# Moving two of five modulation jobs from the projections into attention, and the order of the weight slabs that goes with it

## The reference

```python
m_lat = jax.nn.silu(c) @ w_mod[l] + b_mod[l]                 # 1024 x 6144: sh1, sc1, g1, sh2, sc2, g2
h = modulate(rmsnorm(x, norm_mix[l]), sh1, sc1)              # needs the first 2048 columns only
proj = h @ w_in[l]                                           # q, k, v, glu, two gates: 1024 x 4608
att = latent_neighbourhood_attention(q, k, v, k_c, v_c, rpb[l])
y = merge_branches(proj, att, conv_w, ..., w_att_out, w_conv_out, w_o)
x_mid = x + g1 * y
...
mod = silu(c_2) @ w_ada_2[l] + b_ada_2[l]                    # second block's six vectors, 1024 x 6144
```

## Time and profile before

| | us |
|---|---|
| median of 3 runs | 3107.19 (3105.99 to 3111.87) |
| the profiled execution | 3105.99 |
| its span in the profile | 3104.0 |
| first job of the kernel starts on TensorE | 36.00 |
| attention starts | 264.50 |
| merge starts | 367.53 |
| TensorE busy | 2247.8 |
| VectorE busy | 1420.5 |

### The profile page before, as it was taken

One profiled execution on the slowest core, in us unless ns is written; L12 is line 12 of the kernel. 1 busy time (PEld: TensorE's weight loads), 2 busy tenths in 40 slices (PEclk: granted clock), 3 DMA queues, 4 the chain that ended last, 5 costly groups with the idle time before them and its releaser, 6 DMA issues.

```text
span 3104.0 us, 28552 instructions
## 1 busy us (share of the span) xinstructions
PE 2247.8 (72%) x9662; PEld 967.5 (31%) x9662; DVE 1420.5 (46%) x3317; ACT 703.3 (23%) x1672; POOL 596.9 (19%) x593
## 2 busy tenths in 40 slices
PE   2998899858877774799778986547765655665554
PEld 1443544433322221354557543212211111111110
DVE  1394411320000002201258566666677777777765
ACT  2003411110000101302146443212222222232222
POOL 1000000010000001000012222243443444444442
PEclk8999999869999997889788688768878777777777
DMA  8348519449999996422036856899999999999996
GB/s 256 126 168 292 207 67 216 191 162 401 404 412 410 412 414 237 163 81 82 28 134 248 323 230 267 314 372 400 417 419 421 421 421 421 421 403 422 421 421 266
DMA packets 216905, 922.69 MB, mean 297 GB/s; under 512 B 19266, under 2 KB 59280, under 8 KB 125902
## 3 DMA queue, kind: packets, MB, share of 16 engines
q0 software_dynamic: 79056, 552.76, 43.8%
q1 hardware_dynamic: 127936, 359.68, 31.4%
q10 hardware_dynamic: 9790, 8.73, 0.8%
HBM read 889.32 MB, written 31.78 MB: 297 GB/s over the span
## 4 chain that ended last, share of the span: by engine, by line
DMA 31%; PE 27%; DVE 12%; issue 4%; ACT 4%; POOL 1%; SPq 0%; DVEq 0%; POOLq 0%; ACTq 0%
DMA ring<-in_expert_pair,ids 16%; DMA ring<-in_w_exp_up 11%; PE bank L1883 7%; PE bank L2423 5%; PE bank L2105 5%; DVE ring L1832 4%; PE bank L1889 3%; DMA arena_v<-in_expert_pair,ids 1%; DMA pair_last<-in_expert_pair,ids 1%; PE bank L2436 1%; ACT arena_w L1277 1%; DMA ring<-in_w_exp_down 1%; PE bank L2239 1%; PE bank L2238 1%; DVE pair_last L1832 1%
## 5 line engine op out<-in xcount | busy, mean ns | idle before, releaser
L2423 PE MATMUL bank<-ring,arena_w 128*32 128x512 f32 x1568 | 552.6, 828 | 360.9 <-ACT arena_w L1277 360.9
L873 POOL DMA_INDIRECT ring<-in_expert_pair,ids x392 | 421.4, 1075 | 1139.1 <-PE bank L2423 706.5
L1883 PE MATMUL bank<-arena_h,ring 128*128 128x512 f32 (+1 forms) x1024 | 372.4, 524 | 4.9 <-ACT arena_h L916 2.5
L2105 PE MATMUL bank<-ring,arena_h 128*64 128x512 f32 x1056 | 272.7, 675 | 81.3 <-DMA ring<-in_w_exp_up 74.5
L2423 PEld LDWEIGHTS bank<-ring,arena_w 128*32 128x32 f32 x1568 | 94.3, 132 | 675.4 <-ACT arena_w L1277 507.9
L1832 DVE CUSTOM_DVE_ANT_0 ring<-ring,arena_h 128x1024 f32<-128x1024 f32 x203 | 245.7, 1226 | 126.2 <-DMA ring<-in_expert_pair,ids 91.4
L1832 DVE CUSTOM_DVE_ANT_0 ring<-ring 128x1024 f32<-128x1024 f32 x189 | 229.6, 1225 | 76.9 <-DMA ring<-in_expert_pair,ids 68.3
L1883 PEld LDWEIGHTS bank<-arena_h,ring 128*128 128x128 f32 x1024 | 178.7, 197 | 187.9 <-issue 182.0
L1578 DVE TENSOR_TENSOR arena_q<-arena_q,bank 128x256 f32<-128x256 f32 x32 | 13.5, 421 | 488.7 <-ACT arena_q L1045 488.7
L1275 ACT ACTIVATE arena_w<-arena_w 128x2 f32<-128x2 f32 (+1 forms) x224 | 45.4, 203 | 761.7 <-DVE arena_w L1832 761.4
L2105 PEld LDWEIGHTS bank<-ring,arena_h 128*64 128x64 f32 x1056 | 94.4, 154 | 258.0 <-issue 250.7
(11 more groups left out here) (451 smaller groups left out, 3058.4 us busy)
## 6 DMA issues: line engine op xcount, KB each, us to landing
ring<-in_w_exp_gate SPq DMA_DIRECT2D x33, 2048.0 KB, 19.4
ring<-in_w_exp_up SPq DMA_DIRECT2D x33, 2048.0 KB, 23.6
ring<-in_w_exp_down SPq DMA_DIRECT2D x33, 2048.0 KB, 24.3
ring<-in_w_in SPq DMA_DIRECT2D x15, 2048.0 KB, 19.2
ring<-in_w_mod SPq DMA_DIRECT2D x12, 2048.0 KB, 16.4
ring<-in_w_ada SPq DMA_DIRECT2D x12, 2048.0 KB, 14.8
xs_d<-zeros SPq DMA_DIRECT2D x1, 12032.0 KB, 69.9
arena_h<-xs_d SPq DMA_DIRECT2D x66, 128.0 KB, 23.3
```

Of the source, the lines that this page charges most:

```text
L873: pool.indirect_dma_start(pair[pair_of(m)], None, A["expert_pair_2"], bass.IndirectOffsetOnAxis(ap=ids[n % 2][:, r:r + 1], axis=0)).then_i ...
L1883: mm = pe.matmul(dst, w[:, c, at], rhs[:, c, :], start=(c == 0), stop=(c == chunks - 1))
L2105: mm = pe.matmul(bank[2 + b][at, :].rearrange("p (g f) -> p g f", g=2), xbT[b][:, c, :], gu[:, :, c, 256 * half:256 * half + 256], start=( ...
L2423: mm = pe.matmul(bank[4 + 2 * (n // H % 2) + half][at, :], sel_q[:, n % 2, k0 + j, :], pair[pair_of(m + j)][:, D + 512 * half:D + 512 * ha ...
```

## The change

J0 moves from behind projection 7 to behind projection 10. J1 and J2 leave the projections; the four jobs J1 to J4 stand behind steps 4, 8, 11 and 14 of attention, all in bank 7. The slabs are listed as K, V, Q (6, 7, 8) and then the twenty of the jobs in a row (J0 9 to 12, J1 13 to 16, J2 17 to 20, J3 21 to 24, J4 25 to 28); from 29 on the list is unchanged. VectorE adds J0's bias behind the whole convolution. On GpSimd's queue each later bias load trades places with a store of rows.

```diff
-        jobs = [(cols_pc(A["w_mod"], 4 + j), (DC, 512), pe_mod, 2 + j // 4) for j in range(8)]
-        jobs += [(cols_pc(A["w_ada_2"], j), (DC, 512), pe_mod, 4 + j // 4) for j in range(12)]
-        slabs += [(cols_pc(w_in, QKV + 1), (DC, 512), proj_done, 8)] + jobs[0:4]
-        slabs += [(cols_pc(w_in, QKV + 2), (DC, 512), proj_done, 14)] + jobs[4:8]
-        slabs += [(cols_pc(w_in, QKV), (DC, 512), proj_done, 18)] + jobs[8:20]
+        slabs += [(cols_pc(w_in, QKV + 1), (DC, 512), proj_done, 8), (cols_pc(w_in, QKV + 2), (DC, 512), proj_done, 14),
+                  (cols_pc(w_in, QKV), (DC, 512), proj_done, 18)]
+        slabs += [(cols_pc(A["w_mod"], 4 + j), (DC, 512), pe_mod, 2 + j // 4) for j in range(8)]
+        slabs += [(cols_pc(A["w_ada_2"], j), (DC, 512), pe_mod, 4 + j // 4) for j in range(12)]
...
-        N_JOB = (7, 12, 17, 21, 25)
+        N_MOD, N_GLU, N_K, N_V, N_Q, N_JOB, N_GA, N_WO = 0, 4, 6, 7, 8, 9, 29, 35
...
-        PROJ_JOB, AT_MEAN, AT_VAR, AT_JOB = (7, 13, 17), 0, 2, (4, 9)
-        JOB_BANK = (0, 1, 2, 7, 7)
+        PROJ_JOB, AT_MEAN, AT_VAR, AT_JOB = 10, 0, 2, (4, 8, 11, 14)
...
             bias_rows(0)
             store_rows(0)
+            bias_rows(1)
             store_rows(1)
-            bias_rows(1)
+            bias_rows(2)
             store_rows(2)
-            bias_rows(2)
+            bias_rows(3)
             store_rows(3)
-            bias_rows(3)
             store_rows(4)
...
-                if cc >= 2:
-                    job_rows(cc - 2)
-            job_rows(2)
+            job_rows(0)
...
-                    job_rows(3 + AT_JOB.index(i - 1))
+                    job_rows(1 + AT_JOB.index(i - 1))
...
-                if m in PROJ_JOB:
-                    j = PROJ_JOB.index(m)
+                if m == PROJ_JOB:
                     pe.wait_ge(u_done, CC)
-                    modulation(N_JOB[j], JOB_BANK[j], 0 if j < 2 else 2)
+                    modulation(N_JOB, 0, 0)
...
-                if i == 1:
-                    pe.wait_ge(mod_rows, 4 + 12)
...
-            pe.wait_ge(mod_rows, 4 + 8)
+            pe.wait_ge(mod_rows, 4 + 4)
...
-                    j = 3 + AT_JOB.index(i)
-                    if j == 3:
+                    j = 1 + AT_JOB.index(i)
+                    if j == 1:
                         pe.wait_ge(cms_done, 1)
                     else:
                         pe.wait_ge(mod_rows, 4 + 4 * j)
-                    modulation(N_JOB[j], JOB_BANK[j], 2)
+                    modulation(N_JOB + 4 * j, 7, 0 if j < 2 else 2)
```

More of the change, by code:

```diff
@@ L490, in build @@
         slabs += [(cols_cp(A["w_o"], j), (DC, 512), wo_pe, 8) for j in range(2)]
-        N_MOD, N_GLU, N_K, N_V, N_Q, N_GA, N_WO = 0, 4, 6, 11, 16, 29, 35
-        N_JOB = (7, 12, 17, 21, 25)
+        N_MOD, N_GLU, N_K, N_V, N_Q, N_JOB, N_GA, N_WO = 0, 4, 6, 7, 8, 9, 29, 35
         def w_gu(w, e):
@@ L1390, in job_rows @@
                     dve.wait_ge(*((mod_out_rest, 64 * i) if i <= 2 else (mod2_out, 64 * (i - 2))))
-                dve.tensor_tensor(mod_row, bank[JOB_BANK[i]][:, :], mod_bias[i % 3], ALU.add).then_inc(mod_rows, 4)
+                dve.tensor_tensor(mod_row, bank[7 if i else 0][:, :], mod_bias[i % 3], ALU.add).then_inc(mod_rows, 4)
             dve.wait_ge(convw_T, CC)
```

## The result

Six runs of the changed kernel had a median of 3126.52 us (3119.99 to 3131.48), six of the kernel before one of 3109.53 (3104.42 to 3122.53). The ratio is 1.0055, with a 95% interval from 1.0033 to 1.0078: 17 us, somewhere between 10 and 24. The forecast had the direction (slower, near the bound) and the mechanism, the ring running dry, and it was too small: 3115.0 with a range to 3122. All 23 executions of the changed kernel, seventeen of them outside this comparison, have a median of 3129.77 (3119.99 to 3143.69).

The account below looks back on a forecast made before the run. TensorE, gapless before attention and from the merge on, bounds the kernel, so the merge's start sets the end. Merge 7.5 us late plus 1.5 for the clock, 9.0 on 3105.99, gave 3115.0 us, range 3101 to 3122.

Parts of the forecast that it names:

- the ring running dry: Six-slot ring in attention: late slabs freed only by the preceding job make J3, J4 and merge wait, 12.1 us in all.
- wait ahead of J3, J4, merge: TensorE's waits for late ring loads in attention and at the merge's start: 4.2, 4.2 and 3.7 us.
- the later merge is found again: Behind the merge nothing swallows a shift, so its later start moves the experts and the end by the same amount.
- GpSimd's reordered bias loads cost nothing: Bias loads queued behind row stores in attention: the 1.3 us wait at step 8 lies under J2's 7 us.
- TensorE's clock. I take 1.5 in all: Slow clock behind the three new load waits: bounds 0 and 2.3 us each, 1.5 us taken in all.
- the backlog of loads would partly swallow a slower J3: In attention, a slower J3 is partly swallowed by queued loads; the start of the merge is not.
- I take 15.5: From a job's end to its batch's second slab landing, ahead of J3 and J4: 15.5 us, from readings of 15.5 and 16.7.
- by the backlog: Ahead of the merge: slab 30 lands 26.8 us behind J3, the next two 10.9 us later, at 375.1.
- The sum: Whole kernel: 7.5 + 1.5 = 9.0 us on the profiled execution's 3105.99, giving 3115.0.
- The loads in time: Rival: second slab within 11.3 us, no load waits, merge 4.6 us early, 3101.4; loads in time or nearly, chance 0.22.
- Attention swallowing the jobs: Rival: attention's 26 us of TensorE idle takes the moved jobs, up to 14 us kept, 3092; below 3101, chance 0.08.
- Everything at its upper bound: Rival: longest load times and low-clock jobs, merge 13.5 us late, 3119.5; above 3121 with later stages slower, chance 0.08.

Follow-up runs that it names:

- half: Changed kernel with J2, J3 and J4 loading two slabs each instead of four, same 64 matmuls; ratio 0.9987 to the kernel before, attention stretch 134.47 us.
- shift110: Kernel before with 128 extra unused matmuls directly ahead of the merge; 110.3 us later at the merge, ratio 1.0359.
- shift14: Kernel before with 32 extra unused matmuls directly ahead of the merge; they took 27.7 us, ratio 1.0060.
- warm: Changed kernel with 3, 4 and 6 unused matmuls in the load waits ahead of J3, J4 and the merge; ratio 1.0029 to the kernel before.
- split: Changed kernel with the wait for the two output weights moved behind the merge's first gate matmuls; ratio 1.0029 to the kernel before.
- spaced: Changed kernel with J3 and J4 one step later, behind steps 12 and 15 of attention; ratio 1.0048 to the kernel before.
- one_moved: Kernel before with only J2 moved from the projections into attention, its three jobs there behind steps 4, 8 and 12; ratio 0.9993.
- gap: Kernel before with J2 moved into TensorE's wait ahead of the variance and J3 put behind step 5; ratio 0.9985.

## Why the prediction was right in kind and too small

| step of the forecast | forecast | measured |
|---|---|---|
| attention starts | 250.5 | 250.53 |
| J1, J2 start | 278.5, 307.8 | 278.32, 307.48 |
| J3 could start, starts | 326.1, 330.3 | 327.81, 331.02 |
| wait ahead of J3, J4, merge | 4.2, 4.2, 3.7 | 3.21, 4.13, 6.58 |
| job's end to second slab in use (J3, J4) | 15.5, 15.5 | 16.5, 15.6 |
| J3, J4 last | 7.1, 7.1 | 8.7, 8.7 |
| J4's end to the merge | 15.0 | 15.9 |
| merge starts | 375.0 and a part of 1.5 | 379.90 |
| merge's first 32 matmul records, beyond 14.0 | rest of the 1.5 | 1.4 |
| total | 3115.0 | 3126.52 |

**What held.** The ring running dry, step by step: which slab is held by which job, three waits and none ahead of J1 and J2, the landing 16.4 and 15.4 us behind a job's end. `half` takes only slabs away and all of the loss goes. That the later merge is found again: the first experts' matmul comes at 685.55 and not at 670.61, and in the total `shift110` shows it; `shift14` leaves it open to 9 us. That attention starts at 250.53 and not elsewhere is in part luck (below, third).

That GpSimd's reordered bias loads cost nothing held as well. VectorE does wait for them, twice, which it did not in the kernel before:

```profile
306.43 1.04 DVE L1428 TENSOR_TENSOR arena_w<-spare,band 128x512 f32<-128x512 f32 x1 [1.26 <-DMA spare<-skew_d]
...
330.36 1.02 DVE L1428 TENSOR_TENSOR arena_w<-spare,band 128x512 f32<-128x512 f32 x1 [3.02 <-DMA spare<-skew_d]
...
340.95 0.43 DVE L1439 TENSOR_TENSOR bank<-bank,arena_w 128x256 f32<-128x256 f32 x1 [8.74 <-PE bank L1982]
```

The first wait is the forecast's 1.3 us and lies under J2. (The 0.5 us an issue in that sum is 0.54 rounded down and not up, as it says there; the four stores took 1.95 us.) The second, 3.02 us, lies under TensorE's own wait for J3's slab, and VectorE then waits 8.74 us for TensorE's next scores. `half` has both too (1.16 and 2.51 us), without the loss.

**What failed, first: the term "TensorE's clock. I take 1.5 in all".** It lay between bounds of 0 and 2.3 for each of three waits, so 0 to 6.9, and I chose near the lower end. Measured are 8.77 - 7.07 = 1.7 behind each of the first two waits and 15.36 - 14.00 = 1.4 behind the third: 4.8. The granted clock of the changed kernel in 330 to 340 us, the stretch of J3, with TensorE busy for 9 of 10 us (columns: PE, PEld, DVE, ACT, POOL, PEclk, DMA share, GB/s):

```profile
330.00:340.00 10.00, 8.98 (x66) 3.10 (x68) 1.79 (x3) 0.00 (x0) 0.00 (x0) 0.83 1.04 383
```

0.83 is the mean of a stretch at 1.2 GHz and the rest at 2.4: an estimate from it is a third of the 10 us at the lower level, which costs 1.7 us, as J3 does. The Trainium skill, "TensorE: Matmul & The Clock Gate", section "Part 1: The HAM clock gate", says that the slow clock is the default and that activity releases it; by that `warm`, which only adds activity, should bring the jobs back to their length, and it did (7.07 us). My rows could have said so: the variance had lost 2.28 us behind a wait of 4.93.

I had also argued that the backlog of loads would partly swallow a slower J3. It swallowed nothing: J4's slab 28 is released by J3's end, and J4 starts 15.4 to 16.2 us behind that end in five traces (the changed kernel's two, `split`, `warm`, `spaced`), however late it is.

**Second: what loads took.** "I take 15.5" was the lower of two rows, 15.5 and 16.7. J3 came 16.5 us behind J2's end, 1.0 us more; J4 was as forecast. For the last load, "by the backlog" I let slab 30 land 26.8 us behind J3 and the output weights 10.9 later. It landed 26.1 behind (344.4 + 21.4), and the output weights took 13.9 more, to 379.7. From J4's end to the merge that is 15.9 us and not 15.0: 0.9 us.

**Third, smaller.** J2, when it stood behind the last projection, covered ScalarE's copy of it: 0.95 us that I had left out. The table hides it, by luck: the gated unit starts at 75.62 in this execution and not at 76.40, 0.8 us earlier.

The four terms, 3.3 of the clock, 1.0, 0.9 and 0.95, less 0.5 for a J2 that came sooner behind attention's start and for rounding, are the 5.6 us between the forecast's 9.0 and the 14.6 at the merge.

Behind the merge, `w_o` took 57.99 us where it took 56.72:

```profile
551.12 57.99 PE L1884 MATMUL bank<-ring,arena_q 128*128 128x512 f32 x128 [4.80 <-DVE arena_q L1473]
```

The wait of 4.80 us ahead of it is in both kernels; it is the clock behind it that differs (0.71 in the changed kernel's 551 to 561, 0.83 in 537 to 547 of the kernel before). Whether the change does this isn't shown, and it is unlikely: 56.7 us stand in `half`, `warm`, `spaced` and `shift14`, 57.8 to 58.2 in the other seven, among them `shift110` and `one_moved`, which are made from the kernel before.

**Fourth: the base.** The sum was made on one execution, 3105.99, and three runs with a median of 3107.19. Three more runs put that median, now of six, at 3109.53; 32 beside the first variants had 3115.18. With 14.6 at the merge 3109.5 gives 3124.1, and 3125.4 with the 1.3 of `w_o`, where 3126.52 was measured. So of the 11.5 us between forecast and result, 3.5 are the base, 5.6 the terms above, and the last 2.4, with `w_o` in them, are not told apart from the spread.

**The rivals.** The loads in time: not so, but `half` shows that the price would have been -2.3, not -4.6. The three steps behind J2 take 13.2 us there (13.3 in the changed kernel, 314.48 to 327.81) and not the 11.3 that I had read behind the old J4; those behind J3 take 11.4, those behind J4 with the last copy 10.3. That is 1.0 us more in all; the way to J2 and the jobs themselves add 0.4, and ScalarE's copy behind the last projection 0.95. Attention swallowing the jobs: only where it waits anyway; a job in its second half costs 4.5 us with `one_moved`, one ahead of the variance 0.55 with `gap`. Everything at its upper bound, 3119.5: closest to what came, with 13.5 us at the merge for the 14.6, and 4.9 us of the clock for the 4.8.

## What to carry to other kernels

In a ring of n slots, moving a consumer moves the moment at which the slab n places later is asked for; follow each slab to the consumer that frees its slot and compare the way between the two with the measured time from issue to landing, the second of a batch and not the first. The load waits of TensorE of 2.6 to 13.7 us in these traces cost themselves and another 1.4 to 2.5 us of slow work behind them, and in a chain of loads freed by that work this was paid at each link. Work moved off a full stretch was nearly free only where a wait already stood: one such place took a job for 0.55 us, and the next job cost as much as it had saved.

## What the runs showed of the hardware

- Behind waits of 3.21, 4.13 and 6.58 us the next 64 matmul records took 8.77, 8.77 us (7.07 without a wait) and the next 32 longer ones 15.36 (14.00). Filling the pause with matmuls of no use removes it (7.07, 7.07 and 13.97 in `warm`). The extra did not grow with the wait: 2.5 us behind 2.55 in `spaced`, 1.4 behind 6.58.
- An fp32 matmul of 128x512 with 128x128 weights stands in the trace as two records of 0.43 us: 32 calls gave 64 records and 27.7 us. The 64 matmuls of a job are records too, of 32 calls in the kernel.
- The total of one kernel varies from 3097 to 3128 us, although its start repeats to about 3 us (attention at 264.50, 261.79 and 262.96 in three traces of the same code). One place where it varies is the first stage of experts, where the DMA engines are full: 542.8 us from its first matmul to its last in the profiled execution before, 563.5 in the changed kernel's, 551.2 to 561.1 in the eleven others, whatever stood ahead of them. The other is what follows that stage: 1876 to 1891 us. The two traces in 700 to 1150 us, same columns as above:

```profile
700.00:1150.00 450.00, 356.68 (x1470) 131.97 (x1468) 22.85 (x54) 42.63 (x81) 0.00 (x0) 0.92 1.02 409
```

```profile
700.00:1150.00 450.00, 355.01 (x1444) 130.37 (x1440) 22.06 (x53) 42.03 (x80) 0.00 (x0) 0.91 1.02 397
```

409 GB/s in the kernel before and 397 in the changed one, with the DMA engines as full (1.02) in both. The experts' stage is 20.7 us longer, which makes the difference between the two profiled spans, 33 us, twice that of the medians. Why the rate differs between executions no run here shows.
